# Delta rule: two tiles in flight, and X and R of the backward direction on the other chunk's partitions

## The reference

```python
# per head (4), per direction (2), per chunk of 64 tokens; all in float32
gc = cumsum(g);  decay = where(i >= j, exp(gc_i - gc_j), 0)
lower = where(i > j, (kb @ k.T) * decay, 0)        # kb = k * beta
a = lower + I                                      # 64 x 64, unit triangular
u = solve(a, v * beta);  w = solve(a, kb * exp(gc))
attn = (q @ k.T) * decay
# scan over chunks:
v_new = u - w @ S;  o = (q * exp(gc)) @ S + attn @ v_new
S = S * exp(g_last) + (k * exp(g_last - gc)).T @ v_new
```

## Time and profile before

| | |
|---|---|
| median of 3 runs | 2181.34 us (2177.48 to 2181.59) |
| the profiled execution | 2174.96 us, its span 2173.3 us, mean granted clock of TensorE 0.906 |
| PE matmul busy | 1818.2 us, 84% |
| PE weight loads busy | 1486.2 us, 68% |
| DVE, ACT, POOL busy | 986.5, 601.3, 1020.9 us |
| the delta stage's products L885 | 8 of 40 slices of the span hold them, in two bands |

### The profile page before, as it was taken

How to read it: one execution, slowest core, us unless ns; L and a number is a source line. 1 busy time by engine, 2 the same in 40 slices (tenths; PEclk the granted TensorE clock), 3 DMA queues, 4 the chain that set the end, 5 groups by cost and what they waited for, 6 DMA issues and landing times. The chain is left out here.

```text
span 2173.3 us, 49655 instructions
## 1 busy us (share of the span) xinstructions
PE 1818.2 (84%) x21724; PEld 1486.2 (68%) x21724; DVE 986.5 (45%) x1338; ACT 601.3 (28%) x1168; POOL 1020.9 (47%) x912
## 2 busy tenths in 40 slices
PE   4389799979996899969843897999799968999697
PEld 1288799968985555527622887999699855555276
DVE  0635324535535677651106343244355356776411
ACT  0312211133331354451003122111333313444510
POOL 0500376056752577873205004860666525778732
PEclk8589899989997799989965898999899977999899
DMA  7210112210000001022262111122100000010222
GB/s 252 87 59 21 62 40 71 82 38 14 10 4 19 6 18 42 10 102 78 78 238 88 58 32 50 41 70 82 38 14 9 4 19 6 18 42 10 102 78 78
DMA packets 70994, 117.80 MB, mean 54 GB/s; under 512 B 10096, under 2 KB 42096, under 8 KB 70768
## 3 DMA queue, kind: packets, MB, share of 16 engines
q1 hardware_dynamic: 69840, 114.18, 15.8%
q10 hardware_dynamic: 928, 0.34, 0.1%
HBM read 95.03 MB, written 19.47 MB: 53 GB/s over the span
## 5 line engine op out<-in xcount | busy, mean ns | idle before, releaser
L87 PE MATMUL ps<-h_hi,in_w_hi 128*128 128x384 f32 (+1 forms) x816 | 277.2, 340 | 36.6 <-DVE in_w_lo L459 36.6
L1347 POOL TENSOR_TENSOR attn_accp<-attn_accp,attn_pr 128x1024 f32<-128x1024 f32 x112 | 268.8, 2400 | 51.7 <-ACT attn_pr L1401 46.0
L88 PE MATMUL ps<-h_lo,in_w_hi 128*128 128x384 f32 (+1 forms) x816 | 276.0, 338 | 0.0
L89 PE MATMUL ps<-h_hi,in_w_lo 128*128 128x384 f32 (+1 forms) x816 | 275.8, 338 | 0.0
L1542 DVE TENSOR_REDUCE attn_ql<-ps 128x1 f32<-128x1152 f32 x128 | 172.9, 1356 | 133.1 <-PE ps L1458 132.6
L1401 ACT ACTIVATE attn_pr<-ps 128x512 f32<-128x512 f32 x292 | 159.7, 596 | 196.3 <-PE ps L1494 194.6
L87 PEld LDWEIGHTS ps<-h_hi,in_w_hi 128*128 128x128 f32 (+1 forms) x816 | 151.5, 186 | 41.4 <-DVE in_w_lo L459 37.4
L850 POOL TENSOR_TENSOR delta_ML<-delta_EA,local 128x256 f32<-128x256 f32 x180 | 129.5, 744 | 96.5 <-PE ps L885 96.4
L1119 DVE TENSOR_TENSOR delta_TR<-delta_TR,ps 128x512 f32<-128x512 f32 x144 | 98.5, 687 | 122.9 <-PE ps L885 122.8
L88 PEld LDWEIGHTS ps<-h_lo,in_w_hi 128*128 128x128 f32 (+1 forms) x816 | 151.4, 186 | 3.9
L89 PEld LDWEIGHTS ps<-h_hi,in_w_lo 128*128 128x128 f32 (+1 forms) x816 | 151.2, 185 | 3.9
(11 more groups left out here) (238 smaller groups left out, 4040.1 us busy)
## 6 DMA issues: line engine op xcount, KB each, us to landing
mod_w<-in_w_mod SPq DMA_DIRECT2D x12, 2048.0 KB, 12.4
in_w<-in_w_in SPq DMA_DIRECT2D x22, 1024.0 KB, 6.1
gates<-in_gate SPq DMA_DIRECT2D x48, 192.0 KB, 1.9
attn_gt<-gates SPq DMA_DIRECT2D x34, 256.0 KB, 2.6
out_w<-in_w_out SPq DMA_DIRECT2D x16, 512.0 KB, 6.7
out_y<-out_y SPq DMA_DIRECT2D x10, 512.0 KB, 2.9
delta_GB<-gc_rows SPq DMA_DIRECT2D x36, 128.0 KB, 2.9
norm_x<-out_y SPq DMA_DIRECT2D x9, 512.0 KB, 3.4
```

The costliest lines, as they stand in the source:

```text
L87: nc.tensor.matmul(out, a_hi(i), b_hi(i), start=(i == 0), stop=False)
L88: nc.tensor.matmul(out, a_hi(i), b_lo(i), start=False, stop=False)
L89: last = nc.tensor.matmul(out, a_lo(i), b_hi(i), start=False, stop=(i == n - 1))
L1347: nc.gpsimd.tensor_tensor(acc, a, pr[:, n % 4], ALU.add).then_inc(pool_added, 1)
```

## The change

The delta stage alone is changed. The operations stay the same ones, with these differences:

- In direction 1, R and X are kept on the other chunk's partitions (`both_products`: the input half is `c ^ (d & at)`, the output half `c ^ (d & to)`). With direction 0 on the same half and direction 1 across, the x and T products of both directions use all four 64x64 tiles, issued as one group. The R products of levels 1 to 4 stay on the two diagonal tiles.
- DVE makes R0 of direction 1 in a new step, `cross`, with two operations of 64 partitions, where POOL had one of 128. At level 5, DVE's subtraction of direction 1 is two operations of 64 partitions, and it writes to slot 0, on the normal half.
- One semaphore counts both directions' x products, one the T products and one the y products. R of direction 1 waits for the T products.
- The levels of two tiles alternate: levels 4 and 5 of tile j, levels 1 to 3 of tile j+1, and the start of tile j+2. There is one turn more, and `pool_order` gives POOL the same interleaving. `TR` has three buffers, X two and `ML` four for each direction; `kgn` and `diag` have one. The banks of X and Y are now those of the tile (`2 * jj + d`).

```diff
-TURN = [("x1", 0), ("uw0", -1), ("gb", 1), ("y1", 0), ("uw1", -1), ("x2", 0), ("kq", 1), ("ex", 1), ("y2", 0),
-        ("gpq0", -1), ("x3", 0), ("gram", 1), ("y3", 0), ("gpq1", -1), ("x4", 0), ("y4", 0), ("t00", 1),
-        ("x5", 0), ("t01", 1), ("y5", 0), ("au", -1)]
+TURN = [("gb", 2), ("x4", 0), ("x1", 1), ("gpq0", -1), ("y4", 0), ("y1", 1), ("ex", 2), ("gpq1", -1), ("x5", 0), ("x2", 1),
+        ("au", -1), ("y5", 0), ("kq", 2), ("y2", 1), ("gram", 2), ("x3", 1), ("uw0", 0), ("cross", 2), ("uw1", 0), ("y3", 1),
+        ("t00", 2), ("t01", 2)]
+FILL = [("mask", 1, 2), ("mask", 0, 5), ("scale", 0, 0), ("mask", 1, 3), ("scale", 0, 1), ("mask", 1, 4),
+        ("diag", 0, 0), ("diag", 0, 1), ("first", 2, None), ("mask", 2, 1)]
...
-    for j in range(STEPS + 1):
+    for j in range(-1, STEPS + 1):
...
+                def both_products(phase_of, at, to, out, lhs, rhs):
+                    for h in range(NDH):
+                        for d in phase_of:
+                            for c in range(2):
+                                a, b = rows(c ^ (d & at)), rows(c ^ (d & to))
+                                last = nc.tensor.matmul(out(d)[b, h, :], lhs(d)[a, h, :], rhs(d)[a, h, :], start=True, stop=True)
+                    return last
...
                     elif name[0] == "x":
...
-                            chunk_products(d, 0, lambda r, h: ML[d][r, i % 2, h, :],
-                                           lambda r, h: TR[d][r, jj, 0, h, :]).then_inc(x_mm[d], 1)
+                        pe.wait_ge(ml_done, 2 * nth_mask[j, i])
+                        last = both_products(range(2), 0, 1, lambda d: heads(2 * jj + d), lambda d: ML[d][:, jj, i % 2],
+                                             lambda d: TR[d][:, j3, 0])
+                        last.then_inc(x_mm, 1)
                     elif name[0] == "y":
...
+                        pe.wait_ge(x_out, 2 * nth[j, i])
+                        if i < 5:
+                            both_products(range(2), 1, 0, lambda d: heads(2 * jj + d), lambda d: TR[d][:, j3, 1],
+                                          lambda d: X[d][:, jj]).then_inc(t_mm, 1)
+                            for d in range(2):
+                                if d == 1:
+                                    pe.wait_ge(t_mm, nth_t[j, i])
+                                last = both_products([d], 1, 1, lambda d: heads(2 * jj + d, 4 * CHUNK), lambda d: X[d][:, jj],
+                                                     lambda d: TR[d][:, j3, 1])
+                        else:
+                            last = both_products(range(2), 1, 0, lambda d: heads(2 * jj + d, 4 * CHUNK), lambda d: X[d][:, jj],
+                                                 lambda d: TR[d][:, j3, 1])
+                        last.then_inc(y_mm, 1)
...
+                    elif name == "cross":
+                        dve.wait_ge(half_done, j + 1)
+                        for c in range(2):
+                            last = nc.vector.tensor_tensor(
+                                TR[1][rows(1 - c), j % 3, 1], local[rows(c), L_ID, :].unsqueeze(1).broadcast_to([CHUNK, 4, CHUNK]),
+                                TR[1][rows(c), j % 3, 0], ALU.subtract)
+                        last.then_inc(r0_done[1], 1)
...
+                                for c in range(2):
+                                    last = nc.vector.tensor_tensor(tr[rows(c), 0], tr[rows(1 - c), 1],
+                                                                   heads(2 * jj + 1, 4 * CHUNK)[rows(c)], ALU.subtract)
+                                last.then_inc(y_out[1], 1)
```

More of the change, by code:

```diff
@@ L707, in delta_order, with pool_order, level_counts @@
                 phase(j + ahead, name)
+def pool_order(phase):
+    phase(0, "first", None)
+    phase(0, "mask", 1)
+    for j in range(-1, STEPS):
+        for name, ahead, i in FILL:
+            if 0 <= j + ahead < STEPS:
+                phase(j + ahead, name, i)
+def level_counts():
+    done = {}
+    delta_order(lambda j, name: done.update({(j, int(name[1])): len(done) + 1}) if name[0] == "x" else None)
+    kept = {}
+    delta_order(lambda j, name: kept.update({(j, int(name[1])): len(kept) + 1}) if name in ("y1", "y2", "y3", "y4") else None)
+    masked = {}
+    pool_order(lambda j, name, i: masked.update({(j, i): len(masked) + 1}) if name == "mask" else None)
+    return done, kept, masked
 def turn_tile(j):
@@ L749, in delta_rule @@
         EA = both("EA", [P, 3, 2, 2, 2, CHUNK])
-        TR = both("TR", [P, 2, 2, 4, CHUNK])
-        X, ML = both("X", [P, 4, CHUNK]), both("ML", [P, 2, 4, CHUNK])
-        kgn, kdb, qg = (both(n, [P, 2, 4, HD]) for n in ("kgn", "kdb", "qg"))
+        TR = both("TR", [P, 3, 2, 4, CHUNK])
+        X, ML = both("X", [P, 2, 4, CHUNK]), both("ML", [P, 2, 2, 4, CHUNK])
+        kdb, qg = (both(n, [P, 2, 4, HD]) for n in ("kdb", "qg"))
+        kgn = both("kgn", [P, 4, HD])
         UW = both("UW", [P, 2, 4, HD])
-        diag = both("diag", [P, 2, 2, 2, CHUNK])
+        diag = both("diag", [P, 2, 2, CHUNK])
         S = both("S", [P, S_CTX + 1, 2, HD])
@@ L793, in place @@
             return 2 * (h % 2) + h // 2
+        nth, nth_t, nth_mask = level_counts()
         with nc.Block() as block:
@@ L846, in mask_level @@
                         if i >= 3:
[L847 to L850, removed]
+                            pool.wait_ge(x_mm, nth[j, i - 2])
+                        elif j >= 2:
+                            pool.wait_ge(x_mm, nth[j - 2, 5 if i == 1 else 4])
@@ L859, in first_level @@
-                    pool.drain()
[L860 to L878, removed]
+                        if j >= 3:
+                            pool.wait_ge(uw_mm[d], j - 2)
@@ new lines, in first_level @@
+                        last = nc.gpsimd.tensor_tensor(pairs(TR[d][:, j % 3, 1 - d]), EA[d][:, j % 3, :, 0], level_mask(0, d), ALU.mult)
+                        if d == 1:
+                            last.then_inc(half_done, 1)
+                    pool.drain()
+                    r0 = TR[0][:, j % 3, 1]
+                    nc.gpsimd.tensor_tensor(r0, local[:, L_ID, :].unsqueeze(1).broadcast_to([P, 4, CHUNK]), r0,
+                                            ALU.subtract).then_inc(r0_done[0], 1)
@@ L880, in _, with phase @@
+                def phase(j, name, i):
+                    if name == "first":
+                        first_level(j)
+                    elif name == "mask":
+                        mask_level(j, i)
+                    elif name == "scale":
+                        scale_tokens(j, i)
+                    else:
+                        diagonal(j, i)
+                pool_order(phase)
             @block.tensor
```

85 lines of the change are left out of this document (42 added, 43 removed).

## The result

| | median | runs |
|---|---|---|
| before, on the same chip | 2179.41 us | 6 (2173.60 to 2184.44) |
| after | 2192.73 us | 6 (2184.78 to 2196.05) |
| ratio | 1.0063 | 95% interval 1.0043 to 1.0082 |

The change makes the kernel slower by 0.6%: 13 us, where 3.8 us less were forecast. The time lies in the stated range (2160 to 2198), on the other side of before than the forecast. The profiled execution of after took 2194.09 us (span 2192.4, clock 0.899), 19.1 more than that of before.

What follows compares the result with a forecast made beforehand. PE was taken as bound by tiles and instruction supply at nearly the same pace; filling 16.3, turns 165.2, 9.4, end 10.2 and cross 0.2 gave 201.3 against 203.2 us a layer, -3.8 in two, so 2178 us, range 2160 to 2198.

Steps and rivals of the forecast that it cites:

- rival D: New x and T products: the four tiles do not overlap, turns of 22.0 in place of 21.5, 2186 us; chance 0.04.
- rival A: Delta stage: instruction supply is no bound, turns take 17.5 us, 2121 us in all, or 2138 with today's standing; chance 0.09.
- the gain of the faster products: PE's turn: four tiles cut its demand by 4.6 us, spent standing for instructions; 0.1 us a turn is left.
- my sign of error: Profile after the change: a PE that waits for DVE or POOL rather than for issue would make the forecast wrong.
- the supply term: PE's instruction stream: 5.83 blocks of 256 instructions a turn at 3.68 us, 21.5 us, sets the turn.
- walked the turn: One turn in the new order, followed by latency: 17.5 us, with PE waiting 2.1 of them.
- the forecast's 165.2: Turns 0 to 7 of a layer: 44.9 blocks at 3.68 us, 165.2 us.
- the filling: Start of each layer's delta stage: 16.3 us, between 15.0 and about 22 if the clock stays at half.
- turn 8 and the end: Last part of each layer's stage: 9.4 us up to the last subtraction, then an unchanged 10.2 to the last copy.
- Rival B: PE's instruction supply: PE starves harder, a block costs 3.89 us, 9.4 us a layer more, 2197 us; chance 0.24.
- turning point: Price of a block of instructions from which the slower rival decides, where filling and turns balance: 3.72 us.

Runs made afterwards that it cites:

- e9: The kernel before with gram computed five times over, 256 PE instructions more a tile: 2241.01 us, ratio 1.0307 to before.
- e6: The changed kernel with 72 more waits a tile in PE's program, on semaphore values long reached: 2190.86 us, ratio 1.0077 to before.
- e7: The changed kernel with its turn in another order (kq ahead of y5, au behind y5, uw0 ahead of x3): 2192.26 us, ratio 1.0085 to before.
- e2: The changed kernel with gram computed twice, 64 PE instructions more a tile: 2198.12 us, ratio 1.0121 to before.
- e8: The changed kernel with matmuls merged (160 PE instructions fewer a tile) and its turn in another order: 2160.10 us, ratio 0.9927 to before.
- e4: The kernel before with matmuls that share weights merged, 160 PE instructions fewer a tile: 2147.20 us, ratio 0.987 to before.
- e5: The changed kernel's four-tile products and cross, but one tile in flight, in the order and filling of before: 2241.07 us, ratio 1.0315 to before.
- e11: The kernel before with gram five times, the four extra rounds moving 8 columns in place of 64: 2242.51 us, ratio 1.0320 to before.

## Why the prediction was wrong

**Right.** Four tiles run x and T at 15 ns a record; rival D is out. The blocks are 256 instructions, 44.9 of them in turns 0 to 7 (45 packets): from 513.35 to 532.28 the trace of before holds 632 loads, 631 matmuls and 17 semaphore instructions of PE, which is 1280, 5x256, and in six turns of after's layer 0 28 of the 29 stands for instructions of 0.2 us and more lie 256 recorded instructions, or a multiple of that, apart (to one). In neither trace does a packet of q8 start under 2.29 us after the end of the last, or under 3.30 us after its start; outside the delta stages the starts lie up to 66.9 us apart. No request for a block is recorded, so when one is made is not shown. The instructions supplied, not the tiles, pace PE, before and after (e9: 2.1 us of tile work more, 3.94 us of turn); rival A (17.5 us turns) is out: no even turn of after was under 21.3. `cross` cost DVE 2 x 893 ns a turn, for the 2 x 752 that I took, and nothing on the path. That the gain of the faster products would be spent standing for instructions is what happened (4.2 us a turn; I had said 5 or more). A PE that waits for DVE was my sign of error, though "rather than for issue": it does both.

**The step that failed** is the supply term, and in it this sentence: "That exceeds 17.5 and sets the turn". I had walked the turn and found that PE waits 2.1 us in it for operands. I had priced the supply at 5.83 x 3.68 = 21.5. Then I took the larger of the two and put the waits at nothing. The turns measured 22.63 and 22.71 (from x4 to x4), 3.88 and 3.90 a block. The nearest sum, 21.5 and the measured waits of 1.43, is 22.9. Over turns 0 to 7 the forecast's 165.2 became 179.05 and 177.0, which is nearly the whole of the miss; PE waited 2.3 + 8.6 + 2.1 = 13.0 us for operands there in layer 0. That this fits so well is in part luck, as the single blocks show.

From the start of one packet of the instruction queue q8 to the start of the next is one block. In turns 0 to 7 of both layers of after there are 88 such intervals, mean 3.92 us:

| wait for an operand in the interval | intervals | mean us |
|---|---|---|
| none | 51 | 3.79 |
| begins less than 1 us behind the packet's start | 16 | 3.71 |
| begins 1 to 2.5 us behind it | 12 | 4.17 |
| begins 3.3 to 3.6 us behind it | 4 | 5.36 |
| begins 3.8 us or more behind it, and lasts past the next start | 5 | 4.11 |

The same count in e6 gives 3.75, 3.71, 4.24 and 4.96 for the first four rows, in e7 3.80, 3.72, 4.25 and 5.53. A wait that begins with the packet cost nothing (3.71, to 0.20); one that begins when the next packet is about due cost about twice its length (waits of 0.67 to 0.95 us). Weight loads of PE behind stands for instructions: a block of 3.73 us without a wait, from 550.94 on; one of 5.42 us with such a wait, from 554.67 on; and one of 3.43 us with a wait that cost nothing, from 594.36 on:
```profile
550.94 1.01 PEld L1035 LDWEIGHTS ps<-delta_UW,delta_EA 64*64 64x64 f32 x32 [1.54 <-issue]
...
554.67 0.19 PEld L922 LDWEIGHTS ps<-delta_TR,delta_X 64*64 64x64 f32 x4 [0.23 <-issue]
...
556.40 0.59 PEld L922 LDWEIGHTS ps<-delta_TR,delta_ML 64*64 64x64 f32 x32 [1.05 <-DVE delta_TR L1172]
...
560.09 0.24 PEld L913 LDWEIGHTS ps<-delta_kgn,delta_TR 64*64 64x64 f32 x5 [1.40 <-issue]
...
594.36 0.13 PEld L940 LDWEIGHTS ps<-delta_EA,delta_UW 64*64 64x64 f32 x2 [0.76 <-issue]
...
596.07 1.01 PEld L1035 LDWEIGHTS ps<-delta_UW,delta_EA 64*64 64x64 f32 x32 [0.35 <-DVE gq L1186]
...
597.79 0.43 PEld L922 LDWEIGHTS ps<-delta_TR,delta_X 64*64 64x64 f32 x20 [0.47 <-issue]
```
Against 3.79 the waits of the table cost (12 x 0.38 + 4 x 1.57 + 5 x 0.32 - 16 x 0.08) / 2 = 5.6 us a layer, less than half of the 13 waited. The other part of the miss is the price of a block without a wait: 3.79 (95% interval 3.69 to 3.89) in place of 3.68 is 4.9 us a layer. By the same count before has 3.75 (3.68 to 3.82) in the even turns, so this part need not be an effect of the change: 3.68 was somewhat low for before too.

The other terms, layer 0 / layer 1: no run shows the 16.3 us that the sum has for the filling, 0.6 of them for a clock of 0.50; the runs showed 17.1 / 17.7, with a granted clock of 0.50 for 9.7 and 12.4 us of it; turn 8 and the end 19.6 forecast, 19.9 / 18.1. Turn 7 took 25.3 in layer 0 and 22.7 in layer 1. From x3 to x4 it was 8.0 us in layer 0, and 5.4 in layer 1 at a granted clock of 1.00, which is that difference of 2.6. The stretch behind a wait of 1.55 us for DVE, columns as in the earlier trace rows, has a granted clock of 0.50:
```profile
647.13:652.00 4.87, 4.83 (x121) 4.87 (x125) 0.00 (x0) 1.52 (x4) 3.60 (x6) 0.50 0.01 3
```
**Rival B** gave the right side and nearly the right time (2197), and the price by its measure, 3.94 to 3.99, lay over its turning point of 3.72. Its mechanism, that a starved block is itself dearer (3.89), is neither shown nor ruled out: blocks without a wait take 3.79 in after, and 3.90 in e2 and 3.88 in e8 (each to 0.11). Its turning point holds: with the waits in the price, filling is no longer paid for.

**Does the place of a wait matter?** The trace has the start and the end of each packet of q8. In the six turns of after's layer 0 there are 35 blocks. In 30 of them the next packet starts 1.05 to 1.53 us after the block's first instruction, in five 2.10 to 3.20 us after it. The packets last 0.88 to 1.41 us, and where PE stood, it goes on 1.22 to 1.58 us after a packet's end. Three of the five late packets have a wait for DVE of 0.65 to 1.05 us ahead of them, behind the block's first instruction, and start 0.98 to 1.47 us after that wait's end (wait ended at 556.40, packet at 557.87, block begun at 554.67); the other two (2.23 and 2.38 us) have no such wait. Waits that begin less than 1 us behind a packet's start stand beside intervals of 3.71 us. So a late packet often has a wait ahead of it, and need not; what ties the two together is not shown. That packets come late behind some waits and not behind others would fit the table of intervals, and e8, which gave back about half of what it removed. No run moved one wait through a block, so it is not tested. Why blocks without a wait are at 3.9 in e2 and e8 stays open.

## What to carry to other kernels

In this kernel counting PE's instructions told more than counting tiles or columns: one block of 256 more, on four tiles, added 3.94 us to before's turn in layer 0 and layer 1 on average (e9), for 2.1 us of tile work, and merging matmuls that share weights (e4) gave 1.3% where faster products gave nothing (after: 0.6% slower). So make that count, and hold it against the packets of the instruction queue. Nor were the waits that the new order brought free because "there is slack": the 16 intervals with a wait begun less than 1 us behind a packet's start took 3.71 us, the four with one begun 3.3 to 3.6 us behind it 5.36, those without a wait 3.79. Taking the larger of supply and waits was too low by 1.2 us a turn here; their sum was near, but not for every kernel of the table. Two tiles in flight took a turn of the faster products from 25.3 us (e5) to 22.8, and before's 21.6 was shorter than both.

## What the hardware showed that was not expected

- 128 matmuls of 64 columns and 128 of 8 columns cost nearly the same turn (e9, e11: 25.6 and 26.0 us), one block at 3.9 to 4.3 us, with e11's clock at 0.91 to 0.93.
- 72 more waits a tile on reached semaphores made no instruction and no measurable time (e6): they stand on the weight loads, with 174 packets and 2190.86 us as in after (174, 2192.73).
- What stands beside a wait for an operand in after goes by where it begins: less than 1 us behind a packet's start the interval took 3.71 us, 3.3 to 3.6 us behind it (waits of 0.67 to 0.95 us) 5.36, 1.6 us over the 3.79 without a wait.
- Two of after's stages that differ in nothing but the layer differ by 3.3 us: turn 7 by 2.6 and the end by 1.8, both with a lower granted clock in layer 0 (0.87 against 0.92 and 1.00), less 1.1 the other way in filling and turns 0 to 6.
